# Rotary halves exchanged by DMA instead of a TensorE product, and expert weights multiplied unsplit, in a three-layer float32 decoder kernel

## The reference, cut to what matters

```python
def apply_rope(x, cos, sin):
    half = x.shape[-1] // 2
    ...
    x1, x2 = xf[..., :half], xf[..., half:]
    return jnp.concatenate([x1 * c - x2 * s, x2 * c + x1 * s], axis=-1).astype(x.dtype)

def hier_moe(x, w_grp, b_grp, w_exp, b_exp, e_gate, e_up, e_down):
    ...
    for e in range(N_EXPERTS):
        h = jax.nn.silu(xt @ e_gate[e]) * (xt @ e_up[e])
        out = out + (h * comb[:, e:e + 1]) @ e_down[e]
```

## Time and profile before

| | before |
|---|---|
| median of three runs | 2810.83 us |
| the profiled execution, its own time | 2809.1 us |
| its span, first to last instruction | 2807.6 us |
| busy: PE, DVE, ACT, POOL | 94%, 59%, 42%, 5% |
| mean granted TensorE clock | 0.979 |
| DMA queue of SP | 324.15 MB, 32.0% of 16 engines' span |
| DMA queue of POOL (gathers and scatters of 32 expert tiles) | 8.40 MB |
| chain that ended last: PE, DVE, ACT, issue, DMA | 84%, 7%, 5%, 3%, 1% |

### The profile page before, as it was taken

One profiled execution on the slowest core, in us unless ns is written; L12 is line 12 of the kernel. 1 busy time (PEld: TensorE's weight loads), 2 busy tenths in 40 slices (PEclk: granted clock), 3 DMA queues, 4 the chain that ended last, 5 costly groups with the idle time before them and its releaser, 6 DMA issues.

```text
span 2807.6 us, 36515 instructions
## 1 busy us (share of the span) xinstructions
PE 2642.6 (94%) x14834; PEld 1992.0 (71%) x14834; DVE 1647.5 (59%) x2744; ACT 1189.3 (42%) x1815; POOL 138.7 (5%) x101
## 2 busy tenths in 40 slices
PE   6999999999999999999999999999999989989878
PEld 4777677888876786767888887676776758745446
DVE  4698556645446488655645455445435534489767
ACT  3226543423334224653424234345322324388765
POOL 0020000000000020000000000000000000033210
PEclk9999999999999999999999999999999989999999
DMA  3112232232221222233223222312111124599982
GB/s 139 61 64 102 72 124 98 90 104 91 92 89 64 77 74 81 85 109 109 90 90 105 90 91 90 120 55 78 58 49 42 35 95 142 205 382 396 401 335 97
DMA packets 64144, 334.95 MB, mean 119 GB/s; under 512 B 9570, under 2 KB 10338, under 8 KB 31076
## 3 DMA queue, kind: packets, MB, share of 16 engines
q1 hardware_dynamic: 58852, 324.15, 32.0%
q0 software_dynamic: 5120, 8.40, 0.9%
HBM read 312.59 MB, written 28.31 MB: 121 GB/s over the span
## 4 chain that ended last, share of the span: by engine, by line
PE 84%; DVE 7%; ACT 5%; issue 3%; DMA 1%; SPq 0%; POOLq 0%; DVEq 0%; ACTq 0%
PE bank L911 15%; PE bank L913 15%; PE bank L912 15%; PE bank L1091 4%; PE bank L1093 3%; PE bank L1092 3%; PE bank L3212 2%; PE bank L3213 2%; PE bank L3228 2%; PE bank L2310 2%; PE bank L1135 2%; PE bank L1165 1%; PE bank L1155 1%; PE bank L1082 1%; PE bank L2297 1%
## 5 line engine op out<-in xcount | busy, mean ns | idle before, releaser
L911 PE MATMUL bank<-XH,wh 128*128 128x512 f32 x1328 | 530.5, 399 | 13.2 <-DVE XL L1387 8.9
L913 PE MATMUL bank<-XH,wl 128*128 128x512 f32 x1328 | 519.6, 391 | 0.0
L912 PE MATMUL bank<-XL,wh 128*128 128x512 f32 x1328 | 519.5, 391 | 0.0
L1346 DVE TENSOR_TENSOR wl<-raw,wh 128x2048 fp32r<-128x2048 f32 (+1 forms) x165 | 364.0, 2208 | 155.6 <-ACT wh L1878 155.6
L1878 ACT ACTIVATE wh<-raw 128x2048 fp32r<-128x2048 f32 (+1 forms) x165 | 303.4, 1840 | 178.7 <-DMA raw<-in_W 178.6
L911 PEld LDWEIGHTS bank<-XH,wh 128*128 128x128 f32 x1328 | 249.8, 188 | 87.9 <-DVE XL L1387 18.2
L912 PEld LDWEIGHTS bank<-XL,wh 128*128 128x128 f32 x1328 | 250.3, 188 | 53.4 <-issue 3.2
L913 PEld LDWEIGHTS bank<-XH,wl 128*128 128x128 f32 x1328 | 249.9, 188 | 53.9
L911 PE MATMUL bank<-arena_rounded,wh 128*128 128x512 f32 x576 | 230.6, 400 | 5.3 <-DVE arena_rounded L1592 3.2
L912 PE MATMUL bank<-arena_rounded,wh 128*128 128x512 f32 x576 | 229.1, 398 | 0.0
L913 PE MATMUL bank<-arena_rounded,wl 128*128 128x512 f32 x576 | 229.0, 398 | 0.0
(11 more groups left out here) (541 smaller groups left out, 4478.8 us busy)
## 6 DMA issues: line engine op xcount, KB each, us to landing
raw<-in_W SPq DMA_DIRECT2D x153, 1024.0 KB, 4.9
arena<-in_WE SPq DMA_DIRECT2D x40, 1024.0 KB, 25.6
wh_full<-in_WE SPq DMA_DIRECT2D x19, 1024.0 KB, 26.9
raw<-in_WE SPq DMA_DIRECT2D x18, 1024.0 KB, 26.4
gsave<-scr SPq DMA_DIRECT2D x48, 256.0 KB, 2.2
scr<-gsave SPq DMA_DIRECT2D x48, 256.0 KB, 3.8
hT<-in_WE SPq DMA_DIRECT2D x12, 1024.0 KB, 26.3
cst<-in_WE SPq DMA_DIRECT2D x7, 1024.0 KB, 26.9
```

Source lines behind the costliest of these rows:

```text
L911: pe.matmul(ps[0:c.stop - c.start, :], h[:, k, c], hi, start=i == 0, stop=False)
L912: pe.matmul(ps[0:c.stop - c.start, :], h[:, k, c], lo, start=False, stop=False)
L913: mm = pe.matmul(ps[0:c.stop - c.start, :], l[:, k, c], hi, start=False, stop=i == len(xs) - 1)
L1346: w_lo.inc(dve.tensor_tensor(wl[:, i % 3, 0:k], raw[:, i % 3, 0:k], wh[:, i % 3, 0:k].bitcast(F32), ALU.subtract), i)
```

## The change

Rotary part: `rotate` and its PSUM banks are gone. ACT copies every head tile to SBUF (with its gain) behind the square; DVE no longer does. SP issues four DMAs per head tile, 32 partitions (64 KiB) each, which write the exchanged halves into one of three places `RU` (a third one is added); the first waits for the tile and for the rotary work of the tile three before. SP interleaves them with the weight loads. POOL multiplies `RU` by the sines and then the tile by the cosines. The permutation matrix leaves the constants, so the first constant load is 384 columns wide, not 512.

Experts: gate and up are no longer split. The tokens are copied once in float32 (64 columns), and PE makes eight full float32 products of 64 stationary and 512 moving columns, in turn to PSUM rows 0 to 63 and 64 to 127; the two halves are added where high and low were added before. The splits on ACT and DVE are gone, and `XH`/`XL`, which held the high parts, become four more places of the ring: 19. The four are issued together with the two that stood there before. A part is loaded when the part 19 before it has been used, and the ring positions from which the tail takes its places move to 12, 13, 18 (`raw`) and 14, 15 (`hT`). The 68 passes ahead of the tail become 17 products in full float32. Some semaphores are used for a second purpose after the first (`since`).

```diff
@@ -312,7 +315,6 @@
                         bank.plan(("hbr", li, t), 5)
-                    bank.plan(("rot", li, t), 7 if s > 11 and s % 2 else 6)
@@ -584,6 +586,7 @@
         hrec = Signal(sem("hrec"), [(li, g) for li in layers for g in range(4)])
+        halved = [Signal(sem(f"halved{i}_then_e_in{i}"), [(li, t, q) for li in layers for t in range(i, 16, 3) for q in range(4)], 16) for i in range(3)]
         cosd = Signal(sem("cosd"), [(li, t) for li in layers for t in range(16)])
@@ -785,19 +788,17 @@
         YE = [flat(scr[SLOT:128, a:a + 2, :]) for a in (4, 15)]
-        XS = [arr[:, 10240 + 1024 * i:11264 + 1024 * i].rearrange("p (k n) -> p k n", n=128) for i in range(2)]
+        XS = [A3(10240 + 512 * i, 8, SLOT) for i in range(2)]
         HS = A3(14336, 2, SLOT)
-        EH = [flat(x[:, 4 * i:4 * i + 4, :]) for x in (XH, XL) for i in range(2)]
         a_, _ = cparts["cos"]
-        hf, hr = flat(hT[:, :, :]), flat(hTr[:, :, :])
-        RAW = [(raw[:, i, :], wl[:, i, :]) for i in range(3)]
-        WH = [(wh_full[:, i, :], wh[:, i, :]) for i in range(3)]
-        PARTS = ([(A_(12288, 2048), arr[:, 12288:14336])] + [(A_(2048 * i, 2048), arr[:, 2048 * i:2048 * i + 2048]) for i in range(4)] +
-                 [(cst[:, a_:a_ + 2048], cstr[:, a_:a_ + 2048]), WH[0], WH[1], RAW[0], RAW[1],
-                  (hf[:, 2048:4096], hr[:, 2048:4096]), (hf[:, 0:2048], hr[:, 0:2048]),
-                  (A_(8192, 2048), arr[:, 8192:10240]), WH[2], RAW[2]])
-        RAW_AT, HT_AT = (8, 9, 14), (10, 11)
+        hf = flat(hT[:, :, :])
+        RAW = [raw[:, i, :] for i in range(3)]
+        WH = [wh_full[:, i, :] for i in range(3)]
+        XHL = [flat(x_[:, 4 * i:4 * i + 4, :]) for x_ in (XH_full, XL_full) for i in range(2)]
+        PARTS = ([A_(12288, 2048)] + [A_(2048 * i, 2048) for i in range(4)] + [cst[:, a_:a_ + 2048], WH[0], WH[1]] + XHL +
+                 [RAW[0], RAW[1], hf[:, 2048:4096], hf[:, 0:2048], A_(8192, 2048), WH[2], RAW[2]])
+        RAW_AT, HT_AT = (12, 13, 18), (14, 15)
         RING = len(PARTS)
@@ -1071,16 +1064,8 @@
                     if t is not None:
-                        rotate(li, t)
-                    if t is not None:
                         if is_key(t):
                             spread_heads(("hbr", li, t), RT[t % 2], factor((li, t)))
-
-            def rotate(li, t):
-                ps = opened(("rot", li, t))
-                pe.wait_ge(*(bank.empty(("win", li, t))))
-                mm = pe.matmul(ps, C("rot"), head_at(t), start=True, stop=True)
-                bank.filled(mm, ("rot", li, t))
@@ -1298,8 +1283,8 @@
                     if ti == 0:
-                        for i in range(68):
-                            pe.matmul(ps, XH[:, i % 8, 0:128], XL[:, i % 8, :], start=True, stop=True)
+                        for i in range(17):
+                            pe.matmul(ps, XH_full[:, i % 8, 0:128], XL_full[:, i % 8, :], start=True, stop=True)
                     pe.wait_ge(*normed((8, ti)))
@@ -1435,14 +1420,6 @@
                             cuts_to(n0 + (s // 2 if s < 4 else s // 2 + 1) + 2)
-                        key = ("win", li, s)
-                        dve.wait_ge(*bank.full(key))
-                        if s < 3:
-                            bank.emptied(dve.tensor_copy(head_at(s), bank.ap(key)), key)
-                        else:
-                            dve.wait_ge(*hsq((li, s)))
-                            bank.emptied(dve.tensor_scalar(head_at(s), bank.ap(key), K(f"g{HEADS[s][:2]}{li}", 0), None,
-                                                           ALU.mult), key)
                         if s == 4:
@@ -1523,11 +1500,7 @@
                 dst = head_at(t)
-                u = RU[t % 2]
-                key = ("rot", li, t)
-                dve.wait_ge(*bank.full(key))
-                bank.emptied(dve.tensor_tensor(u, bank.ap(key), C("sin"), ALU.mult), key)
-                dve.wait_ge(*bank.empty(key))
+                u = RU[t % 3]
                 dve.wait_ge(*cosd((li, t)))
@@ -1947,9 +1920,13 @@
                             cuts_to(n0 + (s // 2 if s < 4 else s // 2 + 1) + 2)
-                        if s >= 3:
-                            act.wait_ge(*bank.full(("win", li, s)))
-                            hsq.inc(act.activation(HQ[s % 3], bank.ap(("win", li, s)), ACT.Square), (li, s))
+                        key = ("win", li, s)
+                        act.wait_ge(*bank.full(key))
+                        if s < 3:
+                            bank.emptied(act.activation(head_at(s), bank.ap(key), ACT.Copy), key)
+                        else:
+                            hsq.inc(act.activation(HQ[s % 3], bank.ap(key), ACT.Square), (li, s))
+                            bank.emptied(act.activation(head_at(s), bank.ap(key), ACT.Copy, scale=K(f"g{HEADS[s][:2]}{li}", 0)), key)
                     elif s < 20 and s % 2:
@@ -2205,7 +2182,8 @@
                 for t in range(16):
-                    pool.wait_ge(*bank.full(("rot", li, t)))
+                    pool.wait_ge(*halved[t % 3]((li, t, 3)))
+                    pool.tensor_tensor(RU[t % 3], RU[t % 3], C("sin"), ALU.mult)
                     cosd.inc(pool.tensor_tensor(head_at(t), head_at(t), C("cos"), ALU.mult), (li, t))
@@ -2225,6 +2203,16 @@
+            def swap_halves(li, t):
+
+                sync.wait_ge(*bank.empty(("win", li, t)))
+                if t >= 3:
+                    sync.wait_ge(*roped(li, t - 3))
+                src, dst = head_at(t), RU[t % 3]
+                for q in range(4):
+                    a, b = 32 * q, 32 * (q ^ 1)
+                    halved[t % 3].inc(sync.dma_start(dst[a:a + 32, :], src[b:b + 32, :]), (li, t, q))
+
             def gate_out(m, g):
@@ -2255,11 +2243,20 @@
             sync.dma_start(sml[:, :], A["small"]).then_inc(s_in, 16)
-            sync.dma_start(cst[:, 0:512], A["consts"][:, 0:512]).then_inc(c_first, 16)
+            sync.dma_start(cst[:, 0:384], A["consts"][:, 0:384]).then_inc(c_first, 16)
             load_to(0)
-            sync.dma_start(cst[:, 512:n_const], A["consts"][:, 512:n_const]).then_inc(c_in, 16)
+            sync.dma_start(cst[:, 384:n_const], A["consts"][:, 384:n_const]).then_inc(c_in, 16)
             for li in layers:
                 n0 = PER_LAYER * li
+                load_to(n0 + 2)
+                for s in range(20):
+                    if s == 4:
+                        load_to(n0 + 5)
+                    if s % 2:
+                        load_to(n0 + s // 2 + (3 if s < 4 else 4))
+                    t = s if s < 3 else 3 if s == 4 else s - 3
+                    if s != 3 and 0 <= t < 16 and (s < 5 or t > 3):
+                        swap_halves(li, t)
                 for b in range(8):
@@ -3201,25 +3196,20 @@
                 pe.wait_ge(*b.empty(("tok", i)))
-                for q in range(4):
-                    u = 4 * i + q
-                    pe.wait_ge(*moe.lo(u))
-                    h = moe.high(u).rearrange("p (k n) -> p k n", n=512)
-                    l = moe.unit(u, 1).rearrange("p (k n) -> p k n", n=512)
-                    for kk in range(2):
-                        k = 2 * q + kk
-                        if k < 7:
-                            pe.matmul(ps, xs_[:, k, :], h[:, kk, :], start=k == 0, stop=False)
-                        mm = pe.matmul(ps[0:SLOT, :], xs_[:, k, 0:SLOT], l[:, kk, :], start=False, stop=False)
-                    if q == 1:
-                        moe.half.inc(mm, i)
-                        if i > first:
-                            turn(i - 1)
-                mm = pe.matmul(ps, xs_[:, 7, :], h[:, 1, :], start=False, stop=True)
+                for part_ in range(2):
+                    pe.wait_ge(*moe.landed(i, part_))
+                    w = moe.place(i, part_).rearrange("p (k n) -> p k n", n=512)
+                    for kk in range(4):
+                        k, r0 = 4 * part_ + kk, SLOT * (kk % 2)
+                        mm = pe.matmul(ps[r0:r0 + SLOT, :], xs_[:, k, :], w[:, kk, :], start=k < 2, stop=k >= 6)
+                        if part_ == 0 and kk == 3:
+                            moe.half.inc(mm, i)
+                    if part_ == 0 and i > first:
+                        turn(i - 1)
                 b.filled(mm, ("hid", i))
             def down(i):
-                w = moe.place(i, 2)[0].rearrange("p (k n) -> p k n", n=1024)
+                w = moe.place(i, 2).rearrange("p (k n) -> p k n", n=1024)
                 pe.wait_ge(*b.empty(("tur", i)))
@@ -3278,14 +3257,10 @@
-            cuts_to(4 * first + 1)
             tokens(first)
-            cuts_to(4 * first + 3)
             for i in tiles:
-                for q in range(4):
-                    cuts_to(4 * i + q + LEAD)
-                    if q == 1 and i > first:
-                        turned_over(i - 1)
+                if i > first:
+                    turned_over(i - 1)
                 key = ("hid", i)
@@ -3301,21 +3276,6 @@
```

(17 more changed lines are left out.)

49 lines of the change are left out of this document (15 added, 34 removed).

## The result

The changed kernel takes 2793.39 us (median of four runs, 2788.55 to 2794.80) against 2810.81 before: a ratio of 0.9938, 95% interval 0.9923 to 0.9953. It is faster, by 17.4 us where 34.8 were forecast, and lies 1.4 us above the upper end of the range. Its profiled execution took 2793.63 us (span 2792.3), 15.3 us less in span than that of the kernel before, at a mean granted clock of 0.971 (before 0.979).

A forecast was written before the change was run, and what follows sets the result against it. PE was taken as 84% of the chain of waits, the experts as bound by weight arrival. Rotary 25.0, experts and tail 9.6, constants 0.2 sum to 34.8 us off 2809.1; with 1.7 for the median, 2776, range 2764 to 2792.

The forecast's parts named there:

- PE's rotations: First projections: removing 16 rotations of 0.95 us from PE gains 15.2 us per layer.
- Waits in the score steps: First projections: ACT's added copy lengthens three score waits (-1.5), three others improve (+1.1); net 0.4 us lost per layer.
- colder passes 0.3: Start of attention: passes behind the longer wait run at a lower clock, costing 0.3 us per layer.
- 2.0 us of the gain turn into a longer wait there, about 5 us: Start of attention: PE gains 4.8 us, DVE only 2.8, so PE's 3.07 us wait for value copies grows.
- SP and POOL's path: First projections: the DMA exchange and two POOL products fit within two steps, 12.6 us; cost taken as 0.
- at best 5.2: Shortest exchange chain, in us: 0.4 of issue, 2.2 of transfer and 2.6 of POOL products.
- Experts: PE: PE's time per expert falls from 7.41 to 7.1 us, hidden behind weight loading, so worth nothing by itself.
- Four places: Experts' ring: four parts load during idle DMA time, so the last part and loads behind it land 10.6 us sooner.
- So the loads decide the tail's start, not the scatter: Tail: the last loaded block sets its start, moving 10.6 us, while the experts end near 2706 instead of 2723.5.
- the fourth rival: Experts and tail: if the tail's splits were not last, it would start 16 us sooner; 2769 us, chance 7%.
- The colder tail: Tail: PE's wait grows from 2.54 to about 8 us, and colder passes behind it cost 1 us (0 to 4).
- DVE becomes the bound: First projections: DVE, through POOL's products or selection pieces, limits the rotary gain to 12, not 25; 2789 us, chance 10%.

The follow-up runs named there:

- act_order: Changed kernel with ACT issuing the second score eviction and the key tiles' factor ahead of its wait for the step's head tile; 2766.91 us, ratio 0.9848.
- before_order: Kernel before, rotations still on PE, with only ACT's second score eviction and key factor issued ahead of the head-tile wait; 2801.35 us, ratio 0.9991.
- rotary_only: Kernel before with the rotary part of the change alone, gate and up still split, 15 ring places; 2807.84 us, ratio 0.9988.
- ring15: Changed kernel with the ring cut back to 15 places and the 68 passes ahead of the tail as before; 2802.37 us, ratio 0.9975.
- sine_dve: Changed kernel with the sine product moved from POOL to DVE, leaving POOL one product per tile; 2790.47 us, ratio 0.9937.

## Why the prediction was wrong

**PE's rotations** (15.2 per layer): right. In steps without scores or factors a step is 7.21 - 6.39 = 0.82 us shorter, where 0.95 was forecast (13.1 us per layer, not 15.2), and act_order, set against before_order, has 10.8 of the 12.5 us per layer.

**"Waits in the score steps. ... Net -0.4 per layer"**: this is the step that failed. The waits that it lists came out better than forecast, 3.9 us instead of 5.0. What it leaves out cost more. Three things are missing. First, the waits for the factor: the earlier trace rows shows scores only, and I did not ask what the rotation covered in the key steps; four waits of 1.08 us came up there. Second, the low-clock stretch that can follow a wait of 1 us, 1.7 each: with "colder passes 0.3" I priced one place, while the changed kernel had five such stretches between 80 and 160 us, the kernel before one. How many there are changes from kernel to kernel with the same order: in its second layer, and in both of rotary_only's and ring15's, the part from the sum of step 6 to attention took 0.1 to 7.5 us less than the 112.9 of this layer. Third, in ACT's queue, which runs in order, a wait for PE's tile stood ahead of evictions that were ready 5 us before. In layer 1 steps 6 to 10 and 13 to 16 should have shrunk by about 5 us together (five rotations of 0.95) and grew by 5.0.

**"2.0 us of the gain turn into a longer wait there, about 5 us"**: the wait was 8.1 us. The mechanism was right, the size not: DVE did not gain its three sine products, because POOL's products held other DVE operations for 3.6 us. I took that at 0, with a bound of 5 per layer. The rule of the Trainium skill ("SBUF — State Buffer", section "Who interferes with whom"), by which a GpSimd instruction under way blocks a VectorE instruction with two SBUF inputs entirely, agrees with this trace now in both directions: 1.85 us instead of 0.69 beside a product of 1.30 on POOL, and 0.69 again with one product fewer. By the sums it was worth 0.6 to 1.2 us per layer, since moving the product back costs DVE too.

**SP and POOL's path**: right at 0. DVE waited for POOL (13.4 us in layer 1), and PE for neither. The terms were off and the cover large enough: an issue took 0.59 us, not 0.44, a transfer 3.9 from issue to landing, not 2.2, and the "at best 5.2" counts one issue of the four.

**Experts: PE** 7.1: 6.35, hidden as forecast. **Four places** 10.6: 9.6 by ring15.

**"So the loads decide the tail's start, not the scatter"**: wrong, the second step that failed. The last split stands in the earlier trace rows, but ACT waited 3.18 us more for the results of the last expert, and these move by the experts' whole chain, which ended at 2704.0 as forecast (near 2706). That was the fourth rival, with 7%: 16 us where it priced 16, instead of 10.6. The colder tail cost 0.9 behind the first row.

**The stretch in between** was taken as fixed. It moved by 5.0 us against the change in this execution, and by up to 10 in others (1409.5 against 1399.3).

So 25 became 5.1, then 0.0 with the middle stretch, which nobody changed, and 9.6 became 15.3. The total of 17.4 is thus in part luck: by how often the clock fell, the first layers and the middle stretch move by several us between kernels with the same instructions there. The nearest rival in time, "DVE becomes the bound" (2789), had the wrong engine: it was ACT's order, and its time came near the measured one by two errors of opposite sign. That PE's gain stands in the trace of act_order and not in that of the changed kernel settles it. Not tried: the same order with the exchange issued on another queue. Open: why the clock fell five times in one kernel and once in another with equal waits.

## What to carry to other kernels

When work leaves the critical engine, list what that work covered: every wait of this engine on others in the same steps, not the ones with a row of their own alone, and then look in the other engines' queues for ready work behind a wait that it doesn't need. Here moving an eviction and a factor ahead of such a wait was worth more (26.5 us) than the change itself (17.4). A wait of 1 us on TensorE cost about 2.7 where the clock fell behind it; filler products of the same length kept the clock up and were a gain. And after a saturated stretch follow the last result, not only the last load.

## What I had not expected of the hardware

Equal waits don't cost equal time: with 8.2 us of waits for ACT in layer 1, the changed kernel had five stretches of 3.4 us at 1.2 GHz between 80 and 160 us; sine_dve, with the same waits, had one, at 78.53. Within one execution three waits of 1.08 us were followed by one fall. The same untouched code took between 1399.3 and 1409.5 us in the 14 profiled kernels. What decides whether the clock falls behind such a wait stays open. So differences of a few microseconds between kernels of this kind should be read by stage, next to the granted clock, before they are put down to an edit.
